# Last expert piece in two transfers by output half, with half-by-half readout of the slot results

## What is computed

```
y = lax.map(expert, (x_rows, block_e))           # (silu(x @ w_g[e]) * (x @ w_u[e])) @ w_d[e], 32 experts, top 2 per token
x = x + sum over the token's two experts of weight * y
hp = _rmsnorm(x, norm_ple_g)
x = x + (p @ w_ple) * jax.nn.sigmoid(hp @ w_ple_gate)
return _rmsnorm(x, final_norm_g)
```

## Time and profile before

| | us |
|---|---|
| median of three timed executions | 691.74 (690.78 to 692.00) |
| the profiled execution | 692.38 |
| its span in the profile | 690.5 |
| TensorE busy with matmuls | 638.8 (93%) |
| VectorE busy | 380.0 (55%) |
| ScalarE busy | 276.8 (40%) |
| GpSimd busy | 55.5 (8%) |
| mean granted TensorE clock | 0.983 |
| read from memory | 173.17 MB |

### The profile page before, as it was taken

How to read it: one execution, slowest core, us unless ns; L and a number is a source line. 1 busy time by engine, 2 the same in 40 slices (tenths; PEclk the granted TensorE clock), 3 DMA queues, 4 the chain that set the end, 5 groups by cost and what they waited for, 6 DMA issues and landing times.

```text
span 690.5 us, 11099 instructions
## 1 busy us (share of the span) xinstructions
PE 638.8 (93%) x4352; PEld 483.3 (70%) x4352; DVE 380.0 (55%) x666; ACT 276.8 (40%) x429; POOL 55.5 (8%) x81
## 2 busy tenths in 40 slices
PE   7999999999999999999999999899999875768895
PEld 4999997899999999995796888644444431324354
DVE  6686965668777666676767465532222220203285
ACT  6764373465555555545846721401111100010273
POOL 1000000400000000003094600000000000000010
PEclk9999999999999999999999999999999999989999
DMA  9944541747755555105903539999899999999911
GB/s 325 348 140 154 197 153 36 269 157 244 230 189 187 188 189 187 62 0 188 314 2 125 197 142 363 397 426 429 341 432 425 427 427 429 426 425 429 399 64 61
DMA packets 55064, 174.75 MB, mean 253 GB/s; under 512 B 4726, under 2 KB 29426, under 8 KB 48754
## 3 DMA queue, kind: packets, MB, share of 16 engines
q1 hardware_dynamic: 54352, 172.54, 65.3%
q10 hardware_dynamic: 674, 1.69, 0.7%
HBM read 173.17 MB, written 1.05 MB: 252 GB/s over the span
## 4 chain that ended last, share of the span: by engine, by line
PE 67%; DMA 19%; DVE 8%; ACT 3%; issue 2%; another core or an unknown queue 1%; DVEq 0%; ACTq 0%; POOLq 0%; POOL 0%; SPq 0%
PE ps L1779 15%; PE ps L1781 15%; PE ps L1780 15%; DMA arena<-in_w_moe_dram 7%; DMA W<-in_w_ple_gate_dram 7%; PE ps L2294 5%; DMA W<-in_w_moe_dram 4%; PE ps L2354 2%; PE ps L1976 2%; PE ps L2278 2%; PE ps L2401 1%; PE ps L2300 1%; PE ps L2124 1%; DVE arena L1441 1%; PE ps L2075 1%
## 5 line engine op out<-in xcount | busy, mean ns | idle before, releaser
L1779 PE MATMUL ps<-hT_high,w_up_parts 128*128 128x256 f32 x352 | 99.8, 283 | 0.0
L1781 PE MATMUL ps<-hT_high,w_up_parts 128*128 128x256 f32 x352 | 99.6, 283 | 0.0
L1780 PE MATMUL ps<-hT_low,w_up_parts 128*128 128x256 f32 x352 | 99.6, 283 | 0.0
L1779 PEld LDWEIGHTS ps<-hT_high,w_up_parts 128*128 128x128 f32 x352 | 67.5, 192 | 0.5
L1780 PEld LDWEIGHTS ps<-hT_low,w_up_parts 128*128 128x128 f32 x352 | 67.5, 192 | 0.4
L1781 PEld LDWEIGHTS ps<-hT_high,w_up_parts 128*128 128x128 f32 x352 | 67.5, 192 | 0.0
L1272 DVE TENSOR_TENSOR w_up_parts<-W,w_up_parts 128x1024 fp32r<-128x1024 f32 x44 | 52.8, 1227 | 25.1 <-ACT w_up_parts L805 25.1
L805 ACT CAST w_up_parts<-W 128x1024 fp32r<-128x1024 f32 x44 | 44.7, 1046 | 29.4 <-PE ps L1781 29.4
L975 ACT ACTIVATE sg<-ps 128x256 f32<-128x256 f32 x9 | 3.5, 385 | 123.6 <-PE ps L2294 123.6
L1779 PE MATMUL ps<-h_high,dense_high 128*128 128x256 f32 x160 | 45.7, 286 | 0.0
L1780 PE MATMUL ps<-h_low,dense_high 128*128 128x256 f32 x160 | 45.3, 283 | 0.0
(11 more groups left out here) (479 smaller groups left out, 1333.3 us busy)
## 6 DMA issues: line engine op xcount, KB each, us to landing
W<-in_w_moe_dram SPq DMA_DIRECT2D x24, 2048.0 KB, 22.1
arena<-in_w_moe_dram SPq DMA_DIRECT2D x18, 2048.0 KB, 28.1
W<-in_w_up_dram SPq DMA_DIRECT2D x22, 1024.0 KB, 8.6
W<-in_w_in_dram SPq DMA_DIRECT2D x8, 2048.0 KB, 10.9
W<-in_w_down_dram SPq DMA_DIRECT2D x11, 1024.0 KB, 4.9
hh<-in_w_moe_dram SPq DMA_DIRECT2D x4, 2048.0 KB, 30.1
W<-in_w_out_dram SPq DMA_DIRECT2D x2, 2048.0 KB, 8.5
W<-in_w_o_dram SPq DMA_DIRECT2D x2, 2048.0 KB, 8.4
```

The costliest lines, as they stand in the source:

```text
L1779: pe.matmul(o, lhs[0], rhs[0], start=first, stop=False, skip_group_check=True)
L1780: pe.matmul(o, lhs[0], rhs[1], start=False, stop=False, skip_group_check=True)
L1781: return pe.matmul(o, lhs[1], rhs[0], start=False, stop=last_k, skip_group_check=True)
```

## The change

The last expert piece is loaded by two transfers instead of one: first output half 1 (columns 512 to 1023 of each of the four experts), which completes on the ring's semaphore, then half 0, which completes on `frow_landed` (used once before, at the start). On TensorE the products of half 1 for this piece wait for the first transfer and those of half 0 for the second. Of the ten matmuls of 512 columns ahead of the piece two stay, and four of 128 columns stand between the halves. In every step `at_done` now also counts the last product of half 1, and ScalarE copies bank 2 when that has come, and bank 3 when both halves are done; before it waited for both ahead of both copies.

```diff
--- before.py
+++ after.py
@@ -539,8 +539,12 @@
                     sp.wait_ge(sig("downw_used"), ends * DNC + (j - UPC + 1))
                 if n == PLE_AT:
                     sp.dma_start(wple, a["w_ple_2"][0].rearrange("(k p) n -> p k n", p=P)).then_inc(sig(f"ring{n % RING}_landed"), 16)
-                elif n <= NCHUNK:
+                elif n < NCHUNK:
                     load_chunk(n)
+                elif n == NCHUNK:
+                    piece_in, piece_out = (t.rearrange("p (c n) -> p c n", c=COLS) for t in (w_moe[NGRP8 - 1, CPG - 1], ring(n)))
+                    sp.dma_start(piece_out[:, :, 512:D], piece_in[:, :, 512:D]).then_inc(sig(f"ring{n % RING}_landed"), 16)
+                    sp.dma_start(piece_out[:, :, 0:512], piece_in[:, :, 0:512]).then_inc(sig("frow_landed"), 16)
                 else:
                     h = n - NCHUNK - 1
                     sp.dma_start(wpg[h], w_pg[:, :, 512 * h:512 * h + 512]).then_inc(sig(f"ring{n % RING}_landed"), 16)
@@ -973,10 +977,11 @@
 
                 act.wait_ge(sig("upw_used"), n * UPC + 2 * UPC)
                 act.activation(sg, ps[:, 2, 0:F_EXP], ACT.Silu).then_inc(sig("sg_ready"), 1)
-                act.wait_ge(sig("at_done"), n + 2)
+                act.wait_ge(sig("at_done"), 2 * n + 2)
                 act.copy(aT, v3(ps[:, 3, 0:256], 2)).then_inc(sig("aT_ready"), 1)
+                act.wait_ge(sig("at_done"), 2 * n + 3)
+                act.copy(Yp[:, 1, :], ps[:, 2, :]).then_inc(sig("ypb_ready"), 1)
                 act.wait_ge(sig("downw_used"), n * DNC + 2 * DNC)
-                act.copy(Yp[:, 1, :], ps[:, 2, :]).then_inc(sig("ypb_ready"), 1)
                 act.copy(Yp[:, 0, :], ps[:, 3, :]).then_inc(sig("ypa_ready"), 1)
 
             begun = 0
@@ -2345,15 +2350,22 @@
 
                 pe.wait_ge(sig("aT_ready"), n + 2)
                 for f in range(DNC):
-                    if g == NGRP8 - 1 and f == DNC - 1:
-                        for _ in range(10):
+                    last_piece = g == NGRP8 - 1 and f == DNC - 1
+                    if last_piece:
+                        for _ in range(2):
                             pe.matmul(ps[:, 1, :], Yp[:, 1, 0:P], Yp[:, 0, :], start=True, stop=True, skip_group_check=True)
                     landed_chunk(item(CPG * g + UPC + f))
                     for half, bank in ((1, 2), (0, 3)):
+                        if last_piece and half == 0:
+                            for _ in range(4):
+                                pe.matmul(ps[:, 1, 0:P], ident[:], ident[:], start=True, stop=True, skip_group_check=True)
+                            pe.wait_ge(sig("frow_landed"), 32)
                         for c in range(COLS):
                             last = pe.matmul(ps[CAP * c:CAP * c + CAP, bank, :], aT[:, f, CAP * c:CAP * c + CAP],
                                              down_chunk(CPG * g + UPC + f)[:, c, 512 * half:512 * half + 512],
                                              start=(f == 0), stop=(f == 1))
+                        if f == DNC - 1 and half == 1:
+                            last.then_inc(sig("at_done"), 1)
                     last.then_inc(sig("downw_used"), 1)
 
             def pe_step(n, g):
```

## The result

The changed kernel takes 694.85 us (median of 6, 694.07 to 695.72) beside 691.87 us for the kernel before (6, 690.78 to 693.76). The ratio is 1.0029, 95% interval 1.0016 to 1.0043: 2.0 us slower, with 1.1 to 3.0 inside the interval. This ratio is not the quotient of the two medians, which is 1.0043 or 3.0 us, the upper edge of the interval; so the loss is 2 to 3 us. Single executions spread over 1.7 us (changed) and 3.0 us (before), so the difference of two profiled executions is not the result. The profiled execution of the changed kernel took 694.07 us with a span of 692.2.

The account below looks back on a forecast made before the run. The landing of wpg[0] and TensorE's clock after it set the end. Landing +0.57, other parts 0: 692.95 us from the profiled execution, 692.3 from the median; 692.7 taken between, range 691.4 to 694.0.

Parts of the forecast that it names:

- The likeliest case: Whole kernel: time within 0.2% (1.4 us) of the kernel before, chance 0.64.
- rival 1: Idle time before the gate: clock falls earlier and stays low to about 662 or 663; 693.5 us, chance 0.28.
- The transfer: Last expert piece: 2 KB rows instead of 16 KB make wpg[0] land later, +0.57 us.
- Rival 2: Last piece's transfer: row length costs nothing (512-byte rule), so wpg[0] lands as before; 692.0 us, chance 0.14.
- The issue on SyncE: SyncE's queue: one further issue of 4 to 5 us ahead of wpg[0] stays hidden behind queued transfers; cost 0.
- The products and the last readout: Last piece: moe_done 1.2 us earlier, hidden by VectorE's wait for the cast of wpg[0]; worth 0.
- The readout in every step: The other eight readouts: nobody waits for VectorE there; worth 0, within 0.1 us either way.
- The clock: TensorE ahead of the gate: idle 3.4 us instead of 1.6, making a clock fall near 657 nearly sure; low stretch 1.93 us.
- Rival 3: End of the kernel: faster, as moe_done counts or full clock is kept at the gate; 691.0 us, chance 0.08.
- Rival 4: Last piece: half 1 lands only shortly before half 0; end the same, 692.7 us, no chance of its own.

Follow-up runs that it names:

- e2: The kernel before with only the last piece in two transfers of 2 KB rows, TensorE waiting for both ahead of the products: ratio 1.0019, +1.3 us.
- e4: As e2, but the two transfers take two experts each, so rows are 8 KB long: ratio 1.0003 to the kernel before, +0.2 us.
- e6: The changed kernel with VectorE's transposed x put ahead of its low part of the gate matrix: ratio 0.9979 to the kernel before, -1.5 us.
- e7: The changed kernel with twelve unread matmuls in TensorE's idle time ahead of the gate: ratio 1.0002 to the kernel before, +0.1 us.
- e3: The kernel before with only ScalarE's readout half by half in every step: ratio 1.0010, +0.7 us.
- e10: e3 with nine unread matmuls in TensorE's idle time ahead of the gate: ratio 0.9988 to the kernel before, -0.8 us.
- e8: The kernel before with six unread matmuls in TensorE's idle time ahead of the gate: ratio 0.9995, -0.3 us.
- e12: The changed kernel timed once more, unchanged, beside the kernel before: ratio 1.0029, +2.0 us.
- e5: The kernel before with VectorE's transposed x put ahead of its low part of the gate matrix: ratio 0.9982, -1.2 us.
- e9: The kernel before with two of the ten busy matmuls ahead of the last piece instead of ten: ratio 1.0005, +0.3 us.
- e1: The changed kernel with the last piece loaded by one transfer in 16 KB rows again: ratio 1.0010 to the kernel before, +0.7 us.
- e11: e3 with VectorE's transposed x put ahead of its low part of the gate matrix: ratio 0.9976 to the kernel before, -1.7 us.

## Why the prediction was right and wrong

The measured ratio puts the changed kernel at 693.7 us on the scale of the prediction (691.74 x 1.0029 = 693.75), inside the range of 691.4 to 694.0, but 1.1 us above the 692.7 forecast. By the medians it would be 694.7 (691.74 + 3.0), outside the range, and the plain median of the changed kernel, 694.85, is outside too; so the range held by the ratio only. The likeliest case said no measurable change; what came is nearest to rival 1, slower by the clock, priced at 693.5 with a chance of 0.28.

**The transfer: right.** Taken at +0.57 us, measured at 0.53 in the changed kernel and 0.57 in e2. The 512-byte rule of the Trainium skill ("DMA: Bandwidth & Descriptors", Specifications) does not hold for this stream: rows of 2 KB moved at 387 to 388 GB/s where those of 16 KB moved at about 430, and e4's rows of 8 KB cost nothing that can be told. Rival 2 has fallen.

**The issue on SyncE: right in effect, wrong in size.** I allowed 4 to 5 us more. The second of the two new issues took 11.06 us, so that `wpg[0]` was issued 11.6 us later than before (620.23 instead of 608.65), and that of `wpg[1]` took 25.09, as the last section shows. All stayed hidden: `wpg[0]` was first used 34.65 us after its issue began.

**The products and the last readout: right in time, wrong in worth.** The copy of x was forecast 1.2 us earlier; it started at 652.53, in an execution whose first down piece was used 0.53 us later, so at 652.0 on the clock of the execution before, 0.9 earlier. That VectorE's order hides it was right too: 2.22 us of idle time ahead of L1714, and e6 shows the cover by taking it away. The step that failed is the sentence that its worth is 0. What ends earlier ahead of a fixed landing makes TensorE's idle time longer: 0.94 of the 1.45 us by which it grew in the changed kernel are the readout's (the rest is the later landing), and filling that time gives back 1.9 us there (e7). What the readout costs by itself is less sure: filling gives back 1.5 us in e3 (+0.7 to -0.8, e10) and 0.3 us in the kernel before (e8), whose idle time is 0.6 us shorter, but each of these three times has an interval of 0.6 to 0.7 us to each side, so the difference of 1.2 us is barely outside nothing.

**The readout in every step: right.** TensorE is busy without a gap from 456 to 515 in the changed kernel too:

```profile
456.00:515.00 59.00, 59.00 (x475) 27.31 (x468) 16.04 (x31) 6.55 (x14) 0.00 (x0) 1.00 0.96 403
```

**The clock: the mechanism right, the term mis-sized.** The text saw idle time of 3.4 us instead of 1.6 (measured 3.05) and made the fall nearly sure, but put only 0.4 us of it into the sum, by taking 692.7 between 692.3 and 692.95. Measured, the clock's part of the loss is about 1.5 us, give or take 1.2: 2.0 in all, less the 0.5 that stays when the idle time is filled in both kernels (e7 against e8). It came in both of its forms. In the execution of the profile the clock fell at 655.9, before the gate, and stayed low to 662.7, so over about 5 us of work, just as rival 1 has it; in e12's it fell at 657.5, in the gate. Rival 1 gives as the reason for the long low stretch that TensorE shows too little work; that is argued from one stretch of the kernel before, and no run here tested it.

The size went wrong in two places. One is the 0.4 us for a low stretch priced at 1.93, which treats the kernel before as paying for it in about four executions of five. The profiled executions of e2, e3 and e4, with idle times of 1.3 to 2.2 us, had full clock at the gate, where the kernel before, with 1.60, had not; so it may well pay more seldom than I took it to. How often, no run here counts, and those profiles are each of the fastest execution. The other is small: the first eight records take 3.67 us at full clock, not the 3.44 that the chain shows for the last eight, so an execution without the fall saves 1.70 us and not the 1.93 of my sum.

By the Trainium skill ("TensorE: Matmul & The Clock Gate", HAM oscillation) idle time that waits for DMA between groups of matmuls makes the next group start at the low clock. The trace agrees in the profiled execution of the changed kernel, and not in e12's, whose gate began at full clock after 3.03 us of idle time. The same page (What's actually happening) says that the monitor runs free of the kernel. The traces agree: the gate took 6.03 and 5.37 us in two executions of the same changed kernel.

**Rival 3** was right as a mechanism (full clock at the gate gives back what was lost), but the change alone does not bring it about. **Rival 4** did not occur: half 1 landed 2.7 us ahead of half 0 (646.79 and 649.50).

## What to carry to other kernels

Before moving work to an earlier time, find the instruction behind it in its engine's program order: if that waits for a landing, the gain is idle time, and on TensorE idle time ahead of a chain of matmuls can cost clock. Either exchange the order so that the gain reaches the next matmul (e6: 3.5 us), or fill the gap with matmuls that delay nothing (e7: 1.9 us). A transfer that is cut to arrive in parts should be laid out so that its parts still have long rows: the cut itself cost nothing that can be told, the short rows 0.5 us.

## What was not expected of the hardware

One transfer more in a full queue changed SyncE's issue times by far more than one issue. In the changed kernel:

```profile
604.81 4.21 SPq L546 DMA_DIRECT2D arena<-in_w_moe_dram  x1
609.06 11.06 SPq L547 DMA_DIRECT2D arena<-in_w_moe_dram  x1
620.23 0.56 SPq L550 DMA_DIRECT2D W<-in_w_ple_gate_dram  x1
620.90 25.09 SPq L550 DMA_DIRECT2D arena<-in_w_ple_gate_dram  x1
```

Before, the issues took about 4.3 us each, that of `wpg[0]` 4.78 and that of `wpg[1]` 3.96. Here SyncE was held until 646 us. In e4, with one transfer more as well but in rows of 8 KB, the second new issue took 4.84 us and that of `wpg[1]` 31.32. So the 11.06 goes with the short rows, and the long hold at the end with the further transfer. Nothing was queued behind it but the stores of the end, so it cost nothing; what holds it was not tried.

The second thing is the spread: the executions of the unchanged kernel (33 to 35 in each of three sessions) lay between 690.60 and 695.41 us, 3.5 to 4.6 us within a session, which is more than the whole effect of this change. What makes it was not tried, but the profiles show one part. TensorE's clock also falls between 616 and 640 us, in some executions for longer than in others. Where its mean there was 0.93 or more (before, the changed kernel, e2, e3, e5, e6, e8, e9) TensorE was waiting when the first down piece of the last group landed; where it was 0.86 or less (e1, e4, e7, e10, e11, e12) TensorE came late. In e1, with 0.79, it was late enough for the copy of x to end after ScalarE's cast: the gate then had only 0.73 us of idle time ahead of it and started 3.24 us after the cast instead of 3.06. So the idle time ahead of the gate differs between executions of one kernel too, and the times above may be medians over both cases.
